# A multiplier of one held in SBUF and no longer in the instruction: VectorE's two-operand arithmetic in a chain of three transformer layers

## The reference

```
u = rmsnorm(h, g_pre_mix) @ w_in                 # first layer
h = h + rmsnorm(mix(u) @ w_o, g_post_mix)
h = h + rmsnorm(relu(rmsnorm(h) @ w_up)**2 @ w_down, g_post_mlp)
h = h + rmsnorm(sigmoid(h @ w_gate + b) * (p @ w_proj), g_post_ple)

for l in range(2):                               # second and third layer
    u = rmsnorm(x) @ w_in[l]
    x = x + (g0 * conv(u) + g1 * mla(u) + g2 * hgrn2(u)) @ w_out[l]
    x = x + relu(rmsnorm(x) @ w_ff1[l])**2 @ w_ff2[l]

# inside hgrn2, for every head and chunk, with b = cumsum(log f):
A[t, s] = sum_k q[t, k] * exp(b[t, k] - b[s, k]) * k[s, k]      (s <= t)
o = A @ v + (q * exp(b)) @ S
S = exp(b_last) * S + (k * exp(b_last - b)).T @ v
```

## Time and profile before

| | |
|---|---|
| median of 3 runs | 2934.09 us (2927.09 to 2937.89) |
| profiled execution | 2937.56 us, its span 2935.7 us |
| TensorE | 2773.1 us busy, 94% of the span, mean granted clock 0.948 |
| VectorE | 1339.5 us busy, 46% |
| ScalarE, GpSimd | 953.1 us and 916.0 us busy |

### The profile page before, as it was taken

How to read it: one execution, slowest core, us unless ns; L and a number is a source line. 1 busy time by engine, 2 the same in 40 slices (tenths; PEclk the granted TensorE clock), 3 DMA queues, 4 the chain that set the end, 5 groups by cost and what they waited for, 6 DMA issues and landing times.

```text
span 2935.7 us, 43494 instructions
## 1 busy us (share of the span) xinstructions
PE 2773.1 (94%) x16616; PEld 2400.3 (82%) x16616; DVE 1339.5 (46%) x2027; ACT 953.1 (32%) x1514; POOL 916.0 (31%) x396
## 2 busy tenths in 40 slices
PE   7999889999869999999999999989998999999999
PEld 5666668888659999888999999989997777888887
DVE  4443352223357786434352322469675434533222
ACT  3333432223332332434232322332323433333222
POOL 2110234444214322111344433434221113444444
PEclk9998879999879999988999999999999989999999
DMA  4211122222212211101222222222111101222223
GB/s 143 61 54 42 50 76 94 93 93 94 71 42 94 80 51 44 52 31 37 68 91 87 94 87 81 93 78 94 51 51 47 42 29 58 94 94 93 94 97 110
DMA packets 61809, 215.35 MB, mean 73 GB/s; under 512 B 8144, under 2 KB 8144, under 8 KB 61648
## 3 DMA queue, kind: packets, MB, share of 16 engines
q1 hardware_dynamic: 56192, 198.80, 20.7%
q10 hardware_dynamic: 5024, 12.82, 1.4%
q0 software_dynamic: 432, 1.43, 0.2%
HBM read 210.85 MB, written 2.16 MB: 73 GB/s over the span
## 4 chain that ended last, share of the span: by engine, by line
PE 55%; issue 24%; POOLq 12%; DVE 5%; ACT 2%; DVEq 2%; ACTq 0%; DMA 0%; SPq 0%; POOL 0%
PE ps L569 15%; PE ps L570 15%; PE ps L571 15%; POOLq L511 11%; PE ps L659 2%; PE ps L672 2%; PE ps L641 1%; PE ps L935 1%; ACT wh L1073 1%; PE ps L552 1%; PE ps L910 1%; DVE arena L1886 1%; PE ps L780 1%; DVE H L1582 1%; DVE arena L1579 1%
## 5 line engine op out<-in xcount | busy, mean ns | idle before, releaser
L510 POOL TENSOR_TENSOR wl<-stage,wh 128x1024 fp32r<-128x1024 f32 x374 | 907.1, 2425 | 1950.2 <-ACT wh L1073 1949.7
L569 PE MATMUL ps<-Uh,wh 128*128 128x264 f32 (+1 forms) x2768 | 945.8, 342 | 32.1 <-DVE Ul L1585 15.8
L570 PE MATMUL ps<-Ul,wh 128*128 128x264 f32 (+1 forms) x2768 | 909.8, 329 | 0.0
L571 PE MATMUL ps<-Uh,wl 128*128 128x264 f32 (+1 forms) x2768 | 907.7, 328 | 2.2 <-issue 2.2
L1073 ACT ACTIVATE wh<-stage 128x1024 fp32r<-128x1024 f32 x374 | 396.8, 1061 | 1489.7 <-PE ps L571 1487.2
L569 PEld LDWEIGHTS ps<-Uh,wh 128*128 128x128 f32 x2768 | 534.7, 193 | 122.3 <-issue 54.6
L571 PEld LDWEIGHTS ps<-Uh,wl 128*128 128x128 f32 x2768 | 533.4, 193 | 43.3
L570 PEld LDWEIGHTS ps<-Ul,wh 128*128 128x128 f32 x2768 | 535.7, 194 | 39.0 <-issue 1.9
L570 PE MATMUL ps<-HIDl,wh 128*128 128x512 f32 (+1 forms) x1024 | 347.5, 339 | 0.0
L571 PE MATMUL ps<-HIDh,wl 128*128 128x512 f32 (+1 forms) x1024 | 346.3, 338 | 0.0
L569 PE MATMUL ps<-HIDh,wh 128*128 128x512 f32 (+1 forms) x1024 | 346.2, 338 | 0.0
(11 more groups left out here) (292 smaller groups left out, 3323.3 us busy)
## 6 DMA issues: line engine op xcount, KB each, us to landing
stage<-w SPq DMA_DIRECT2D x374, 512.0 KB, 3.3
arena<-bias_rows ACTq DMA_DIRECT2D x16, 448.0 KB, 5.0
arena<-w_mla ACTq DMA_DIRECT2D x8, 384.0 KB, 3.1
H<-xT SPq DMA_DIRECT2D x8, 256.0 KB, 6.6
out<-H ACTq DMA_DIRECT2D x8, 256.0 KB, 2.8
arena<-pT SPq DMA_DIRECT2D x1, 512.0 KB, 8.1
arena<-pairs POOLq DMA_DIRECT2D x1, 512.0 KB, 4.1
arena<-causal POOLq DMA_DIRECT2D x1, 320.0 KB, 3.3
```

Source lines behind the costliest of these rows:

```text
L510: pool.tensor_tensor(wl[:, j, :], stage[:, j, :], wh[:, j, :].bitcast(F32), ALU.subtract).then_inc(w_split, 1)
L569: pe.matmul(dst, w_lead, tok.part(a_lead, h), start=(k == 0), stop=False)
L570: pe.matmul(dst, w_lead, tok.part(a_rest, h), start=False, stop=False)
L571: mm = pe.matmul(dst, w_rest, tok.part(a_lead, h), start=False, stop=(k == len(acts) - 1))
```

## The change

The three helpers read their scalar from the first column of `ones`, a tile of SBUF, where the instruction held the constant 1.0. Values and order of the instructions stay. One wait is added, on DVE before its first work: `consts`, which POOL raises when the constants are written.

```
             def times(dst, a, b):
-                return dve.scalar_tensor_tensor(dst, a, 1.0, b, ALU.mult, ALU.mult)
+                return dve.scalar_tensor_tensor(dst, a, ones[:, 0:1], b, ALU.mult, ALU.mult)

             def plus(dst, a, b):
-                return dve.scalar_tensor_tensor(dst, a, 1.0, b, ALU.mult, ALU.add)
+                return dve.scalar_tensor_tensor(dst, a, ones[:, 0:1], b, ALU.mult, ALU.add)

             def less(dst, a, b):
-                return dve.scalar_tensor_tensor(dst, a, 1.0, b, ALU.mult, ALU.subtract)
+                return dve.scalar_tensor_tensor(dst, a, ones[:, 0:1], b, ALU.mult, ALU.subtract)
...
+            dve.wait_ge(consts, 1)
             dve.wait_ge(vec_in, 32)
```

## The result

| | before | after |
|---|---|---|
| median of 9 runs each | 2931.99 us (2921.78 to 2939.18) | 2948.65 us (2940.90 to 2957.82) |
| profiled execution, its span | 2937.56 us, 2935.7 us | 2944.93 us, 2943.1 us |
| mean granted clock of TensorE | 0.948 | 0.952 |

The ratio is 1.0058, with an interval of 1.0037 to 1.0078: 17 us slower, 11 to 23. The forecast, 2942, was 8.5 us above its before, so the direction was right and the range held the time, but the price was forecast at half of what it is. The two profiled executions are only 7.4 us apart. That is not the change's price: an unchanged copy of the kernel, profiled later, has a span of 2930.2 us, 5.5 us less than the profile of before. I use that copy ("the copy" from here on) beside the first profile wherever two executions of before differ.

A forecast was written before the change was run, and what follows sets the result against it. The prediction took TensorE, with its issue time and POOL's weights, to bound nearly all, DVE some 200 us. Its terms, 4.1 + 4.4 = 8.5 us on the median 2934.09, gave 2942.6, stated as 2942 us, range 2929 to 2954.

The forecast's parts named there:

- the column costs nothing: Rival for all changed instructions: the scalar's place has no price, as in the skill's formula; 2934 us, chance 5%.
- does not wait for POOL: Rival: the column form skips waits for POOL on the path, 17 us faster, 2917 us; chance 6%.
- step 1: Feed-forward, 96 rests: nearly all wait for POOL and DVE idles 1.47 us afterwards, so 0 us.
- steps 2 and 5: Convolution, 12 sums while TensorE has its projections: 0 us; the new wait for `consts`, 3 us in hand: 0 us.
- Step 3: Norms, residuals and sums of squares outside the recurrence, where DVE is the chain: 73 x 0.056 = 4.1 us.
- Step 4: Recurrence, four heads in two layers: waits for POOL swallow most lateness; 2.2 us a layer, 4.4 us, bounds 2 and 10.3.
- The signs of being wrong: Feed-forward rests near 750 ns, POOL's subtractions above 2.9 us, recurrence half-clock stretches above 6.8 us, or unblocked products still 425 ns.
- The case of the forecast itself: Whole kernel: a loss of 3 to 13 us, 2937 to 2947 us, chance 63%.
- Nothing is swallowed: Rival: norms and recurrence pay in full, and blocked instructions pay too; 15.9 us, 2950 us, chance 17%.
- TensorE's clock falls for longer: Rival: longer waits at L873 lengthen the half-clock stretch behind each head; 13.6 us on top of 8.5, 2956 us, chance 9%.

The follow-up runs named there:

- the two kernels without the lock: POOL subtracts 8 columns of each chunk and zero-fills the others; against the kernel before: with the constant 2894.54 us (0.9869), with the column 2898.95 us (0.9898).
- plain: The kernel before with all three helpers written as tensor_tensor, without any scalar: 2928.01 us, ratio 0.9992.
- no_times: The changed kernel with the constant back in the products, so the column in sums and rests alone: 2943.92 us, ratio 1.0032 to the kernel before.
- times_only: The changed kernel with the constant back in sums and rests, so the column in the recurrence's products alone: 2946.19 us, ratio 1.0042 to the kernel before.
- same: The kernel before, unedited, run once more: 2932.02 us, ratio 1.0000.
- level3: The kernel before with the column only in the four products of level 3 in each head: 2922.84 us, ratio 0.9983.
- again: The changed kernel, unedited, run once more: 2947.99 us, ratio 1.0046 to the kernel before.
- levels34: The kernel before with the column only in the eight products of levels 3 and 4 in each head: 2938.45 us, ratio 1.0025.

## Why the prediction was right in part

*What bounds the kernel, and the price of the column: right.* +0.056 us an instruction was read from two pairs of rows and measured at +0.058 to +0.061 over the shapes that never wait (in the two kernels without the lock 690 and 749 ns at 512 columns, 705 and 766 at 528, 434 and 494 at 264, 426 and 485 at 256). The rival "the column costs nothing" falls by the sum H+M, now at 751 ns, and by the ratio's lower end, 1.0037. The Trainium skill (VectorE: DVE Perf Modes, The TRN2 errata) gives (N+151)/0.96 ns for a float32 `tensor_tensor` add, an instruction without a scalar; for 512 columns that is 691 ns. The trace agrees for the form without a scalar (692 in plain) and with the constant (693), and not for the column.

*A blocked instruction waits as before and pays nothing: right.* The feed-forward rests end 0.54 us behind POOL, with a mean of 1729 ns where they had 1734. The rival "does not wait for POOL" (6%) asked for 750 ns there and fell. With it step 1 (feed-forward, 0) and the assumption behind steps 2 and 5 hold; the first instruction of DVE came at 5.18 us, behind its transfer as before.

*Step 3, norms and residuals outside the recurrence, 4.1 us: nothing against it, not confirmed to the us.* Each dearer instruction of a chain shows its 0.06 (the step of 0.68 above, the third layer's 0.5). For the sum, the pair of traces has 1.5 us by 740 and 4.5 by 900, of which up to 1.7 can be the clock's; the two kernels without the lock are 4.4 apart by the medians and 8.5 by the ratios; and `no_times` has 3 to 15. All of these allow 4.1 and none is sharp enough to confirm it.

*Step 4, the recurrence, 4.4 us: wrong, it is about 12 (12.3 by times_only's ratio, 12.4 and 10.8 by the traces).* The sentence that failed is "a DVE instruction that waits for POOL ends at POOL's end however late it came: lateness is swallowed". It is true of an instruction that waits in both kernels. It says nothing of one that started just before POOL and now starts just behind, and that one gains a wait of 2 us for a few tenths of lateness. Three terms show it, with the second layer's numbers in the copy and in the changed kernel:

- Head 0 was put down as "blocked once only, and partly paces TensorE itself, 0.9". It is blocked twice, in products of 2.40 and 2.45 us where it was once in one of 1.10: +2.5. That is with the copy's 6.8 us of half clock at the head's start; against the first profile, which has 3.4 there, it is +3.8. I had rows of the head at 1075 us only and took over its pattern.
- Head 1, forecast +0.24, takes +2.6. Its first 3.4 us run at half clock behind TensorE's wait of 3.58 us: 1.7 lost. In all six column traces of the first head there is such a stretch behind it, of 3.4 us four times and 10.2 twice; in the six of before, same and no_times none. (Both heads of plain and level3 that fell behind POOL have one of 6.8.)
- Head 2 has neither trouble and the pattern of the head that I worked out in full. It takes +1.0 and not +0.24. Here the working itself has a hole. I asked what becomes of kfull, which had come just ahead of POOL, and found it blocked. The one to ask for was the first instruction that now starts behind POOL's start. In the changed kernel's third head, DVE then POOL:

```profile
1138.36 3.00 DVE L1579 SCALAR_TENSOR_TENSOR arena<-arena,ones 128x256 f32<-128x256 f32 x2
1141.44 0.75 DVE L1579 SCALAR_TENSOR_TENSOR HID<-arena,ones 128x512 f32<-128x512 f32 x1
1142.11 0.76 DVE L1579 SCALAR_TENSOR_TENSOR arena<-arena,ones 128x528 f32<-128x528 f32 x1
...
1138.50 2.58 POOL L510 TENSOR_TENSOR wl<-stage,wh 128x1024 fp32r<-128x1024 f32 x1 [6.89 <-ACT wh L1073]
```

and in the copy of before:

```profile
1131.58 0.69 DVE L1579 SCALAR_TENSOR_TENSOR HID<-arena 128x512 f32<-128x512 f32 x1
1132.19 2.88 DVE L1579 SCALAR_TENSOR_TENSOR arena<-arena 128x528 f32<-128x528 f32 x1
...
1131.63 2.87 POOL L510 TENSOR_TENSOR wl<-stage,wh 128x1024 fp32r<-128x1024 f32 x1 [6.89 <-ACT wh L1073]
```

A product of 256 columns ahead of kfull is now the blocked one (the pair of 3.00; kfull is the HID row of 512 columns behind it). Before, qfull waited itself and DVE was through 0.57 us behind POOL's end at 1134.50; now kfull and qfull both stand behind that end (1141.08), and DVE is through 1.79 behind it. POOL, held up less, gives 0.3 back. The remaining 0.2 of the layer's +6.3 is head 3.

*The signs of being wrong.* Two of them came. POOL's subtractions reach 2.97 us twice in the changed kernel (limit 2.9; before, the longest is 2.89), where DVE's L2053 (L2052 before, a column form in both kernels) now starts 0.01 us ahead of POOL. Half-clock stretches of 10.2 us (limit 6.8) stand behind the first head in `again` and `times_only`. And TensorE's waits at L873 did not rise by 0.2 to 0.5 each, as said above.

*Luck.* The case of the forecast itself had 2937 to 2947, a loss of 3 to 13 us; 2948.65 and 17 us lie outside both. The time lies in the stated range because that was widened for the rivals and the spread of the runs.

*The rivals.* "Nothing is swallowed" gave 2950, next to the measured 2948.65, for a reason that the runs refute: blocked instructions pay nothing, and without the lock the recurrence pays nothing at all. "TensorE's clock falls for longer" named a mechanism that takes part, with a wrong place and size: not behind every head but behind the first of each layer, where the wait went from 0.74 to 3.58 us and more. The stretch of the earlier trace rows, behind head 1, is in neither the copy nor the changed kernel; it came and went between executions of the same kernel, and its presence in the first profile is a part of why the two profiles first looked only 7.4 us apart.

What stays open: how much of the loss goes to the new waits and how much to the half clock behind them, and what decides in which executions TensorE's clock is at one half at the start of a layer's first head. The runs show one half in seven of eight such heads of the constant form and two of six of the column's, and no experiment here controlled it.

## What to carry to other kernels

Where two engines exclude each other at a port, a small slowdown is priced by its margin and not by its length: list, for every instruction on the path, how long before the other engine's start it starts, and ask which one is first behind that start once all are later. Here 0.39 us were in hand against 0.06 an instruction: four dearer products a head left it in hand at half clock, and eight did not and gained a wait of 2 us. Ask too how fast the other engine comes to its start: at TensorE's full clock the margin was gone without any dearer instruction. The remedy is on the other engine: cutting POOL's 2.4 us subtraction in four (0.9911, 0.9888 to 0.9934) or in two (0.9923, 0.9897 to 0.9949) gives more than this change lost. With the column as well, the cut in two was not enough: 1.0032.

## What the runs showed of the hardware

- A scalar read from an SBUF column costs VectorE 58 to 61 ns an instruction at 256 to 528 columns (from 426 to 485, from 705 to 766), and nothing where the instruction waits for POOL. A constant scalar and no scalar at all cost the same (434 and 434 ns at 264 columns).
- A fill by POOL (128x1016 columns, 0.94 us, in the kernels without subtraction) does not hold DVE up: the column products of 256 columns stay at 485 ns.
- Cut in two, POOL's subtraction lets a waiting DVE instruction in between its halves: the product then takes 1.3 to 1.6 us, its wait included, and not 2.4 to 2.7, but DVE can be caught twice.
- A TensorE wait of 3.58 us was followed by 3.4 us at 1.2 GHz, one of 5.7 us by 10.2 us (begun while it still waited); those of 0.74 to 1.9 us by none in the copy, though the first profile of before has 6.8 us behind 1.9. The length of the stretch does not follow from the wait alone: in level3 3.54 us were followed by 6.8, in levels34 6.08 by 10.2 and 6.06 by 6.8.
